# Two norms applied behind their projections, a first gather by matrix products, and six convolution taps moved from VectorE

## What is computed

```
for l in range(DEPTH):
    h = rms_norm_2(x, norm1_g[l])
    a, u, v, cv, cg = jnp.split(h @ w_in[l], splits, axis=-1)
    ya = pool_mixer(a, ...)                       # trailing means over 2, 4, 8, 16 tokens
    yb = gmlp_mixer(u, v, ...)                    # u * (W_s norm(v) + b)
    yc = conv_module(cv, cg, ...)                 # GLU, causal depthwise conv of 31 taps, LayerNorm, SiLU, pointwise
    x = x + jnp.concatenate([ya, yb, yc], axis=-1) @ w_out[l]
    h = rms_norm_2(x, norm2_g[l])
    x = x + (swiglu(h, ...) if l == 0 else moe_swiglu(h, router, ...))
return rms_norm_2(x, final_g)
```

## Time and profile before

| | |
|---|---|
| median of the timed runs | 1796.35 us |
| the profiled execution | 1792.17 us |
| its span, first to last instruction | 1790.4 us |
| VectorE busy | 1408.0 us (79%) |
| ScalarE busy | 1145.1 us (64%) |
| GpSimd busy | 231.8 us (13%) |
| second block's mixers | about 388 to 486 us and 684 to 774 us |
| dense block | 495 to 684 us |
| loop over the experts | 808 to 1767 us |

### The profile page before, as it was taken

One profiled execution on the slowest core, in us unless ns is written; L12 is line 12 of the kernel. 1 busy time (PEld: TensorE's weight loads), 2 busy tenths in 40 slices (PEclk: granted clock), 3 DMA queues, 4 the chain that ended last, 5 costly groups with the idle time before them and its releaser, 6 DMA issues.

```text
span 1790.4 us, 27396 instructions
## 1 busy us (share of the span) xinstructions
PE 1697.4 (95%) x10018; PEld 1487.3 (83%) x10018; DVE 1408.0 (79%) x1605; ACT 1145.1 (64%) x1276; POOL 231.8 (13%) x241
## 2 busy tenths in 40 slices
PE   8999899998899999879999999999999999999994
PEld 8888888887899999767888888888888888888883
DVE  7665766769765557957898898898988988989886
ACT  5553655466544446537777777777777777777773
POOL 1212121238000004400010010010100100101000
PEclk9999999999999999889999999999999999999997
DMA  7322532253545364337999999999999999999993
GB/s 297 126 78 80 182 137 83 69 193 135 184 144 188 130 220 139 143 144 285 361 372 395 381 370 380 382 382 367 367 400 380 375 376 377 384 372 365 402 379 141
DMA packets 71473, 477.38 MB, mean 267 GB/s; under 512 B 8421, under 2 KB 9093, under 8 KB 19557
## 3 DMA queue, kind: packets, MB, share of 16 engines
q1 hardware_dynamic: 67781, 463.25, 68.7%
q0 software_dynamic: 3328, 12.08, 1.8%
q10 hardware_dynamic: 288, 1.05, 0.1%
HBM read 470.05 MB, written 6.29 MB: 266 GB/s over the span
## 4 chain that ended last, share of the span: by engine, by line
PE 76%; DVE 9%; issue 8%; ACT 2%; POOL 2%; DMA 1%; SPq 0%; ACTq 0%; DVEq 0%; POOLq 0%
PE bank L444 24%; PE bank L446 23%; PE bank L445 23%; DVE wlo L435 2%; PE bank L1044 1%; DVE bank L1720 1%; ACT whi L430 1%; POOL cacc L2131 1%; DVE msb L1690 1%; PE bank L1016 0%; DVE sm L1610 0%; PE bank L705 0%; DVE rstd L1448 0%; POOL pr L2048 0%; PE bank L978 0%
## 5 line engine op out<-in xcount | busy, mean ns | idle before, releaser
L435 DVE TENSOR_TENSOR wlo<-raw,whi 128x2048 fp32r<-128x2048 f32 (+2 forms) x453 | 999.7, 2216 | 192.7 <-ACT whi L430 191.9
L430 ACT ACTIVATE whi<-raw 128x2048 fp32r<-128x2048 f32 (+2 forms) x453 | 838.2, 1851 | 228.6 <-PE bank L446 228.3
L444 PE MATMUL bank<-whi,hthi 128*128 128x512 f32 x896 | 354.2, 395 | 0.0
L446 PE MATMUL bank<-whi,htlo 128*128 128x512 f32 x896 | 350.1, 391 | 0.0
L445 PE MATMUL bank<-wlo,hthi 128*128 128x512 f32 x896 | 349.7, 390 | 0.0
L444 PE MATMUL bank<-uhi,whi 128*128 128x272 f32 (+2 forms) x1072 | 315.6, 294 | 11.7 <-DVE wlo L435 7.7
L446 PE MATMUL bank<-uhi,wlo 128*128 128x272 f32 (+2 forms) x1072 | 307.3, 287 | 0.0
L445 PE MATMUL bank<-ulo,whi 128*128 128x272 f32 (+2 forms) x1072 | 306.7, 286 | 0.0
L444 PEld LDWEIGHTS bank<-uhi,whi 128*128 128x128 f32 (+1 forms) x1072 | 202.8, 189 | 14.4 <-DVE wlo L435 8.4
L445 PEld LDWEIGHTS bank<-ulo,whi 128*128 128x128 f32 (+1 forms) x1072 | 203.1, 189 | 0.6
L446 PEld LDWEIGHTS bank<-uhi,wlo 128*128 128x128 f32 (+1 forms) x1072 | 202.9, 189 | 0.0
(11 more groups left out here) (341 smaller groups left out, 2109.6 us busy)
## 6 DMA issues: line engine op xcount, KB each, us to landing
raw<-in_wm SPq DMA_DIRECT2D x338, 1024.0 KB, 7.2
raw<-in_w SPq DMA_DIRECT2D x66, 1024.0 KB, 4.9
raw<-in_w SPq DMA_DIRECT2D x18, 768.0 KB, 4.4
raw<-in_w SPq DMA_DIRECT2D x16, 704.0 KB, 4.1
raw<-in_w SPq DMA_DIRECT2D x14, 512.0 KB, 3.7
ys<-y_slots SPq DMA_DIRECT2D x4, 512.0 KB, 5.0
raw<-in_w SPq DMA_DIRECT2D x2, 576.0 KB, 4.6
hT<-in_hT SPq DMA_DIRECT2D x2, 544.0 KB, 5.9
```

The lines of the kernel that those rows point to most:

```text
L430: act.activation(whi[:, n % RING, 0:c], raw[:, n % RAW, 0:c], ACT.Copy).then_inc(hi_ready, 1)
L435: dve.tensor_tensor(wlo[:, n % RING, 0:c], raw[:, n % RAW, 0:c], whi[:, n % RING, 0:c].bitcast(F32), ALU.subtract).then_inc(lo_ready, 1)
L444: pe.matmul(out, s_hi, m_hi, start=start, stop=False, skip_group_check=shared)
L446: return pe.matmul(out, s_lo, m_hi, start=False, stop=stop, skip_group_check=shared)
```

## The change

It does four things.

- The norms ahead of the dense block and the experts are applied behind their projections. Tiles of the residual are scaled by the gain alone as they come (`late_pair`, `late_lo`); the squares are summed by GpSimd and summed over partitions by one product (`row_sum`, `token_sums`). VectorE multiplies the dense gate by the root ahead of SiLU and the down projection's result by the root (the up branch stays unscaled until then). For the experts the root goes into the weights' difference and into the copies to `nt`. Routing steps of two token tiles are joined.
- The first expert's rows are made by products of `nt` with `pick`; the indirect gather remains for the others.
- In the third convolution tile the last six taps are multiplied by ScalarE, added by GpSimd, and their sum added by VectorE.
- The final norm's reciprocal moves behind VectorE's split of PW_U and its products to GpSimd; the two convolution parameters have a semaphore of their own.

```diff
--- before.py
+++ after.py
-N_PAR, PAR2, PAR3, CONST2 = 5, 10, 2, 2
+MOVED = 6
+OWN_TAPS = (TAPS, TAPS, TAPS - MOVED)
+PRODUCTS, PRODUCT_SUMS = TAPS + MOVED, TAPS - 1 + MOVED - 1
+N_PAR, CONV_PAR, PAR2, PAR3, CONST2 = 5, 2, 8, 2, 2
...
+            def row_sum(q):
+                pe.wait_ge(acc_step, q * (KD - 1) + (KD - 1))
+                pe.matmul(bank[7][:, 0:SEQ], mean_d[:], acc[:, 0:SEQ], start=True, stop=True).then_inc(ms_done, 1)
+            def token_sums(q):
+                pe.wait_ge(acc_step, q * (KD - 1) + (KD - 1))
+                for i in range(2):
+                    at = 2 * i
+                    mm = pe.matmul(bank[7][:, at:at + 2], sd[:, i * P:(i + 1) * P], mean_d[:, 0:2], start=True, stop=True)
+                mm.then_inc(ms_done, 1)
...
                 if f >= 2:
-                    pe.wait_ge(fs_ready, t * RAW + (f - 1))
                     pe.wait_ge(fa_ready, t * RAW + (f - 1))
+                else:
+                    pe.wait_ge(xs_ready, XS_PAIR[0] + 3 + f)
...
+                    if f == 0 and k == SUM_AT:
+                        row_sum(FFN_NORM)
...
+            def turn_normed(k):
+                for tt in range(2):
+                    b = bank[2 + 2 * tt + k // 4]
+                    mm = pe.transpose(b[:, (k % 4) * P:(k % 4 + 1) * P], un[:, k, tt * P:(tt + 1) * P], ident[:])
+                    if k % 4 == 3:
+                        mm.then_inc(nt_done, 1)
+            def turn_residual(tt):
+                for half in range(2):
+                    for i in range(4):
+                        mm = pe.transpose(bank[2 * tt + half][:, i * P:(i + 1) * P], xT[:, 4 * half + i, tt * P:(tt + 1) * P], ident[:])
+                    mm.then_inc(xt_done, 1)
             for k in range(KD):
                 pe.wait_ge(un_ready, k + 1)
                 for tt in range(2):
-                    mm = pe.matmul(bank[tt][:, 0:EXPERTS], un[:, k, tt * P:(tt + 1) * P], router[:, k, :], start=(k == 0), stop=(k == KD - 1))
-            mm.then_inc(lg_done, 1)
-            for tt in range(2):
-                for half in range(2):
-                    for i in range(4):
-                        mm = pe.transpose(bank[2 + 2 * tt + half][:, i * P:(i + 1) * P], un[:, 4 * half + i, tt * P:(tt + 1) * P], ident[:])
-                    mm.then_inc(nt_done, 1)
-            pe.wait_ge(chosen_ready, 2)
+                    mm = pe.matmul(bank[6][:, tt * EXPERTS:(tt + 1) * EXPERTS], un[:, k, tt * P:(tt + 1) * P], router[:, k, :],
+                                   start=k == 0 and tt == 0, stop=k == KD - 1 and tt == 1, skip_group_check=True)
+                if k == KD - 1:
+                    mm.then_inc(lg_done, 1)
+                elif k < KD // 2:
+                    pe.wait_ge(xs_ready, XS_PAIR[1] + 3)
+                    turn_normed(k)
+            pe.wait_ge(xs_ready, XS_PAIR[1] + 4)
+            for k in range(KD // 2, KD):
+                turn_normed(k)
+            token_sums(MOE_NORM)
+            turn_residual(0)
+            pe.wait_ge(chosen_ready, 1)
...
+            pe.wait_ge(nt_ready, 2)
+            turn_residual(1)
+            pe.wait_ge(nt_ready, 4)
+            pe.wait_ge(pick_ready, 1)
+            for half in range(2):
+                for i in range(4):
+                    d = 4 * half + i
+                    for tt in range(2):
+                        mm = pe.matmul(first_gathered(half)[:, i * P:(i + 1) * P], nt[:, tt, d * P:(d + 1) * P], pick[:, tt, :],
+                                       start=tt == 0, stop=tt == 1)
+                mm.then_inc(gather_done, 1)
...
+            def late_tile(q, k):
+                act.wait_ge(xs_ready, XS_PAIR[q == MOE_NORM] + k // 2 + 1)
+                out, ready = (un, un_ready) if q == MOE_NORM else (uhi, uhi_ready)
+                act.activation(out[:, k, 0:SEQ], xT[:, k, :], ACT.Copy, scale=gains[:, GAIN_ROW[q], k:k + 1]).then_inc(ready, 1)
+            def late_square(q, k):
+                if k >= 2:
+                    act.wait_ge(acc_step, q * (KD - 1) + max(k - 2, 1))
+                act.activation(sq[:, k % 2, 0:SEQ], xT[:, k, :], ACT.Square).then_inc(sq_ready, 1)
+            def late_pair(q, j):
+                for k in (2 * j, 2 * j + 1):
+                    late_tile(q, k)
+                for k in (2 * j, 2 * j + 1):
+                    late_square(q, k)
...
+                def moved_products():
+                    act.wait_ge(cv_taken, CONV_T * L + CONV_T)
+                    for j in range(MOVED):
+                        k, i = TAPS - MOVED + j, TAPS + j
+                        if j:
+                            act.wait_ge(sum0_done, L * PRODUCT_SUMS + (TAPS - 1 if j < 4 else i - 4))
+                        out = prod[i % 3] if j else csq[:, 1, :]
+                        act.activation(out, hpad[:, CONV_T - 1, k:k + SEQ], ACT.Copy, scale=convw[:, L, CONV_T - 1, k:k + 1]).then_inc(prod_ready, 1)
...
+                moved_products()
                 split_hi(act, n0 + PW_U)
...
                 split_hi(act, n0 + LATE_U + 1)
+                act.activation(warm[:, 6:7], eps[:], ACT.Sqrt)
                 split_hi(act, n0 + LATE_U + 2)
-                split_hi(act, n0 + LATE_U + 3)
+                q = MOE_NORM if L else FFN_NORM
+                for j in range(KD // 2):
+                    late_pair(q, j)
+                    if j == 1:
+                        split_hi(act, n0 + LATE_U + 3)
...
-                act.activation(fs[:, f % 2, :], bank[f % 2][:, 0:SEQ], ACT.Silu).then_inc(fs_ready, 1)
+                act.wait_ge(gate_taken, t * RAW + (f + 1))
+                act.activation(fs[:, f % 2, :], fs[:, f % 2, :], ACT.Silu).then_inc(fs_ready, 1)
...
+            act.wait_ge(ms_done, MOE_NORM + 1)
+            act.activation(sd[:, LEN:LEN + 4], bank[7][:, 0:4], ACT.Sqrt, bias=eps[:]).then_inc(sd_ready, 1)
+            act.activation(warm[:, 6:7], eps[:], ACT.Exp)
+            act.wait_ge(tw_diff, 2)
+            act.activation(tw[:, 1, :], tw[:, 0, :], ACT.Exp).then_inc(tw_exp, 1)
+            act.wait_ge(rstd_ready, MOE_NORM + 1)
...
+                last = tap_sum(c, OWN_TAPS[c] % 2)
...
+                dve.wait_ge(sum0_done, (L + 1) * PRODUCT_SUMS)
+                dve.wait_ge(conv_ready, L * CONV_T + CONV_T - 1)
+                dve.tensor_tensor(cacc[:, CONV_T - 1, :], cacc[:, CONV_T - 1, :], csq[:, 1, :], ALU.add).then_inc(conv_ready, 1)
...
-                            dve.reciprocal(fin[:], fin[:]).then_inc(frs_ready, 1)
-                            dve.wait_ge(xg_ready, KD)
-                            dve.wait_ge(frs_ready, 1)
-                            for k in range(0, KD, 2):
-                                pair = xT[:, k:k + 2, :]
-                                dve.tensor_tensor(pair, pair, fin[:].unsqueeze(1).to_broadcast([P, 2, SEQ]), ALU.mult).then_inc(xs_ready, 2)
...
                 split_lo(dve, n0 + PW_U)
+                if L == 0:
+                    dve.reciprocal(fin[:], fin[:]).then_inc(frs_ready, 1)
...
+                split_lo(dve, n0 + LATE_U + 2)
+                for j in range(KD // 2):
+                    if j % 2:
+                        dve.wait_ge(unit_done, n0 + LATE_U + j // 2 + 1)
+                    else:
+                        dve.wait_ge(out_done, 2 * L + j // 2 + 1)
+                    tiles = xT[:, 2 * j:2 * j + 2, :]
+                    dve.tensor_tensor(tiles, tiles, bank[j][:].rearrange("p (k t) -> p k t", k=2), ALU.add).then_inc(xs_ready, 1)
+                    if L == 0 and j:
+                        late_lo(j - 1)
+                if L == 0:
+                    late_lo(KD // 2 - 1)
+                split_lo(dve, n0 + LATE_U + 3)
+            def late_lo(j):
+                for k in (2 * j, 2 * j + 1):
+                    x_lo(FFN_NORM, k)
+            def x_lo(q, k):
+                dve.wait_ge(uhi_ready, q * KD + k + 1)
+                dve.scalar_tensor_tensor(ulo[:, k, 0:SEQ], xT[:, k, :], gains[:, GAIN_ROW[q], k:k + 1], uhi[:, k, 0:SEQ].bitcast(F32),
+                                         ALU.mult, ALU.subtract).then_inc(ulo_ready, 1)
...
+                dve.tensor_tensor(fs[:, f % 2, :], bank[f % 2][:, 0:SEQ], rstd[:, 0:SEQ], ALU.mult).then_inc(gate_taken, 1)
                 if f:
                     ffn_lo(f - 1, t)
+                dve.wait_ge(fs_ready, t * RAW + (f + 1))
+                dve.tensor_tensor(fa[:, f % 2, :], fs[:, f % 2, :], bank[2 + f % 2][:, 0:SEQ], ALU.mult).then_inc(fa_ready, 1)
...
-                dve.tensor_tensor(xT[:, d, :], xT[:, d, :], bank[4 + d % 3][:, 0:SEQ], ALU.add).then_inc(xs_ready, 1)
+                dve.tensor_tensor(ut[:, d % 2, 0:SEQ], bank[4 + d % 3][:, 0:SEQ], rstd[:, 0:SEQ], ALU.mult).then_inc(down_step, 1)
+                dve.wait_ge(down_step, d + 1)
+                dve.tensor_tensor(xT[:, d, :], xT[:, d, :], ut[:, d % 2, 0:SEQ], ALU.add).then_inc(xs_ready, 1)
...
+                for j in range(1, MOVED):
```

(69 more changed lines are left out.)

189 lines of the change are left out of this document (71 added, 118 removed).

## The result

The changed kernel takes 1773.51 us, median of 4 runs (1772.59 to 1774.14), against 1795.3 us (1793.38 to 1798.51, 4 runs) for the kernel before: ratio 0.988, 95% interval 0.986 to 0.989, 21.8 us less. Forecast were 1771.5 us and 1763 to 1783. The profiled execution took 1772.59 us, its span is 1770.8, 19.6 under that of before.

What follows compares the result with a forecast made beforehand. TensorE, busy 95% of 1790.4 us, bounds the kernel, with waits outside the expert loop. Gains 6.3 + 0.5 + 3 + 15 = 24.8 us give 1767.4 from the profiled execution, 1771.5 us against the median; range 1763 to 1783.

Steps and rivals of the forecast that it cites:

- First mixer: First mixer, split to first output product: final norm off VectorE and early parameters gain 6.3 us (4.5 to 8).
- The second mixer as a picture of the first: The second mixer, 44.73 us without final norm or parameter wait, shows what remains of the first mixer's 51.03 us.
- Final norm on GpSimd: First mixer: the four products on GpSimd and the reciprocal's new place cost nothing, at most 1.5 us.
- My rival: Low clock and blocked sums: holes move but do not close, gain only 18.5 us, 1778 us; chance 0.20.
- Six taps: Third conv tile: moving six taps off VectorE gains 0.5 us (0 to 0.7), in the second layer only.
- Norm ahead of the dense block: Start of dense block: TensorE starts on unscaled tiles but waits at the row sum; gain 2.8, taken as 3 us.
- Dense ring: Dense loop: a VectorE and ScalarE round of 5.17 us hides under TensorE's 5.61 per unit, 0.44 to spare; gain 0.
- the slower rival: Dense loop: the two-engine round overtakes TensorE, 6.97 us a unit, 29 us over 21 units, 1800 us; chance 0.03.
- Norm, routing, first gather: Between second mixer and experts: unscaled tiles and gather by products gain 14.6, taken as 15 us (12 to 18).
- SBUF ports: VectorE and GpSimd alternate on shared ports, delaying GpSimd's sums in splits; total 1769 if squares' sums were free of it.

Runs made afterwards that it cites:

- the second profiles of both kernels: Both kernels profiled again without any edit: the kernel before took 1795.86 us in one execution, the changed kernel 1773.09 us (median).
- three copies: Changed kernel with three ScalarE copies of 256 columns, into buffers nobody reads, added at the end of every dense unit: 1781.44 us.
- the row sum later alone: Changed kernel with the dense norm's row sum behind the first tile of dense unit 1, not behind tile 5 of unit 0: 1769.66 us.
- the three edits: Changed kernel with dense row sum later, final norm's GpSimd products behind the conv tiles' low parts, residual transposes and exponent off the path to the experts: 1764.82 us.

## Why the prediction was right

The sum was 24.8 us and the span fell by 19.6; the profile of before had the early start of the first mixer (398.3 against 400.6 us), and the medians differ by more, 21.8. Of the 3 us missing, 2.3 are the collision below; the rest are small misses both ways, and that they nearly cancel is luck. By steps, the second profiles of both kernels in brackets:

- **First mixer, 6.3 us.** The size was right (5.8 [6.8] between the anchors; 6.5 [7.9] by sigmoid to mean, taps included), its parts were not what the text suggests. The early parameters, named without a price of their own, bring 2.1 us, and the final norm 3.5, though its operations took 5.8 us of VectorE there. The second mixer as a picture of the first stood the test: 45.25 against 44.74 us.
- **Final norm on GpSimd: "nothing, at most 1.5 us".** Wrong, and the one step whose mechanism failed. GpSimd was priced, and VectorE's reciprocal, but not what GpSimd's products do to VectorE: 1.10 us of products became 4.18, and 2.3 [3.8] us of the stage's gain went. My rival had collisions only as a slower GpSimd. Put back, the time was the same.
- **Six taps, 0.5 us, second layer.** The second layer has it (0.4 to 0.8 against the two profiles of the changed kernel). For the first I argued from one profile, in which TensorE reached the mean without idling; in the second profile of before it idles 1.07 us there for VectorE's last sum. The 7.08 us from output product to mean are the same in both, so VectorE set the mean in this layer too, and the taps count there, 0.8.
- **Norm ahead of the dense block, 3 us.** 3.1 [3.6] measured, and the mechanism as written: TensorE idle at the row sum (3.9), sums stretched by the two splits, a low clock behind. The sum ended 9.3 us behind the last output matmul, where 9.8 was forecast. That the lower clock follows each hole is more than the rows say: in the very profile it was read from, the clock stayed at 1.00 behind the hole of 2.5 us near 187 us.
- **Dense ring, 0.** Right; the margin of 0.44 us was near (0.30 by VectorE's wait), and three copies show that the slower rival's mechanism is real from there on.
- **Norm, routing, first gather, 15 us.** 14.1 [12.7] measured from the mean on, 20.6 us behind the last output matmul where 20 was forecast. Parts missed and nearly cancelled, which is luck: the scaled copies ended 0.8 us later than forecast; the products then started 1.1 us behind these copies (0.8 behind `pick`), held by residual transposes ahead of them in TensorE's order, which the forecast had lie beside the routing; and products and select took 5.7 us instead of 7.1, in other profiles of the same code 4.4 to 6.
- **SBUF ports.** The Trainium skill's page "SBUF — State Buffer", section "SBUF: two separate sides", has VectorE and GpSimd take one pair of ports by turns. I had used it in one direction, for GpSimd's sums; the trace shows it in both (VectorE 4.18 against 1.10). The table load again took 1.28 us, and the drain that the Trainium skill's page "ScalarE: Activation LUTs", section "What ACT_TABLE_LOAD costs", adds to it is not seen: in the changed kernel the root's load starts at 475.75 and the next activation at 477.04.

## What to carry to other kernels

Before work is moved to an idle GpSimd, look at what VectorE does in the same microseconds: the price is VectorE's delay and who waits for it. Here the same work 5.7 us later cost nobody a wait. That an engine reaches an instruction without idling in one profile does not say that the instruction's input was early: at the first conv mean the same kernel had no wait in one profile and 1.07 us in the next. And a sum that waits for another engine is better placed in TensorE's order behind independent work than at the first place where it is legal: here one place later gave 3.4 us.

## What the hardware did that I had not expected

- Three VectorE products of 256 columns took 4.18 us beside GpSimd's products of 512 columns, against 1.10 alone: 1.0 us more for each, where one of GpSimd's takes 1.30.
- Behind the same wait of 2.5 us, TensorE's granted clock was 1.00 in one execution of one kernel and 0.77 to 0.80 over the next 8 us in another, worth 1.5 of the 2.4 us by which the first mixer starts later (398.3 or 400.6 us).
- From 495 to 500 us the clock was 0.81 and 0.50 in two profiles of the changed kernel (waits of 1.9 and 3.9 us ahead), 0.73 with the row sum later alone (1.9 and 1.8 us), and 1.00 with the three edits (1.8 us); it was 0.50 too with the final norm back on VectorE, where only the 3.9 us stand ahead. More than this one place I cannot show.
